# The two V products with the meta keys of an attention unit, side by side on 64 rows each, behind the K products

## The reference

```
s_grid = einsum('bqhd,bkqjhd->bhqkj', q_r, k_r) * scale + bias
s_meta = einsum('bqhd,bmhd->bhqm', q_r, km) * scale + mbias
p = softmax(concatenate([s_meta, s_grid], axis=-1))
out = einsum('bhqm,bmhd->bqhd', p_m, vm) + einsum('bhqkj,bkqjhd->bqhd', p_g, v_r)
# layer: h = rms_norm(x); u, g_pool, q, k, v, g_na = split(h @ w_in)
# y = rms_norm(x + concat([pool(u) * silu(g_pool), out * silu(g_na)]) @ w_out)
```

## Time and profile before

| | us |
|---|---|
| runs of the kernel | 1765.36, 1771.95, 1772.95 (median 1771.95) |
| the profiled execution | 1772.99 |
| its span on the slowest core (core 3) | 1771.5 |
| spans of the other cores | 1756.9 to 1767.5 |
| PE busy in the span | 1697.0 (96%) |
| DVE, ACT busy in the span | 1001.9 (57%), 821.2 (46%) |

### The profile page before, as it was taken

How to read it: one execution, slowest core, us unless ns; L and a number is a source line. 1 busy time by engine, 2 the same in 40 slices (tenths; PEclk the granted TensorE clock), 3 DMA queues, 4 the chain that set the end, 5 groups by cost and what they waited for, 6 DMA issues and landing times.

```text
span 1771.5 us, 39313 instructions; the slowest of 8 cores (1756.9 to 1771.5 us)
## 1 busy us (share of the span) xinstructions
PE 1697.0 (96%) x13906; PEld 875.6 (49%) x13906; DVE 1001.9 (57%) x1907; ACT 821.2 (46%) x1219; POOL 114.7 (6%) x186
## 2 busy tenths in 40 slices
PE   7799999999999999999999889899999999999998
PEld 3344544444455555555555554344444444444443
DVE  3354544442466675666667665456655566556654
ACT  3356666331266765677666662223333233323332
POOL 1011021111100000000000110000000000000000
PEclk9899999999999999999999999899999999999999
DMA  9689778653555566666533448853466336642421
GB/s 249 228 221 291 228 238 240 199 169 137 171 138 156 147 177 177 150 185 180 148 108 107 151 133 235 217 140 102 105 173 173 100 92 154 173 138 98 111 95 60
DMA packets 157446, 287.63 MB, mean 162 GB/s; under 512 B 63235, under 2 KB 85251, under 8 KB 148679
## 3 DMA queue, kind: packets, MB, share of 16 engines
q1 hardware_dynamic: 106103, 157.66, 31.3%
q0 software_dynamic: 34880, 91.46, 18.8%
q10 hardware_dynamic: 16272, 35.99, 6.6%
HBM read 193.33 MB, written 100.90 MB: 166 GB/s over the span
## 4 chain that ended last, share of the span: by engine, by line
PE 79%; DMA 6%; ACT 4%; issue 4%; SPq 3%; DVE 3%; ACTq 0%; DVEq 0%; POOL 0%; POOLq 0%
PE bankpair L427 17%; PE bankpair L403 9%; PE bankpair L612 8%; PE bankpair L889 8%; PE bankpair L580 8%; PE bankpair L376 8%; PE bankpair L908 8%; PE bankpair L1016 4%; PE bankpair L985 4%; ACT sb_PT L991 2%; DMA at_s<-sb_ATT 2%; DMA sb_XSG<-xt 1%; SPq L471 1%; SPq L350 1%; PE bankpair L1004 1%
## 5 line engine op out<-in xcount | busy, mean ns | idle before, releaser
L991 ACT ACTIVATE sb_PT<-bankpair 128x1024 bf16<-128x1024 f32 (+1 forms) x368 | 318.9, 921 | 162.7 <-PE bankpair L985 105.8
L427 PE MATMUL bankpair<-sb_Wo,sb_MIX 128*128 128x512 bf16 x1536 | 333.6, 379 | 0.0
L427 PEld LDWEIGHTS bankpair<-sb_Wo,sb_MIX 128*128 128x128 bf16 x1536 | 150.2, 98 | 181.5 <-issue 0.7
L997 DVE TENSOR_TENSOR sb_PT<-sb_PT,sb_FT 128x1024 bf16<-128x1024 bf16 (+1 forms) x264 | 175.4, 667 | 114.0 <-ACT sb_PT L991 111.5
L908 PE MATMUL bankpair<-sb_Wz,sb_HT 128*128 128x512 bf16 x768 | 201.3, 386 | 3.6 <-ACT sb_PM L934 2.8
L580 PE MATMUL bankpair<-sb_HT,sb_Wk 128*128 128x512 bf16 (+1 forms) x832 | 191.2, 385 | 8.3 <-ACT sb_Wk L215 3.9
L889 PE MATMUL bankpair<-sb_HT,sb_Wq 128*128 128x512 bf16 x768 | 191.8, 380 | 1.9 <-DVE sb_QT L213 1.7
L376 PE MATMUL bankpair<-sb_HT,sb_Wg 128*128 128x512 bf16 x768 | 186.4, 387 | 5.9 <-DVE sb_Y L430 4.7
L612 PE MATMUL bankpair<-sb_Wv,sb_HT 128*128 128x512 bf16 x816 | 184.0, 379 | 0.0
L433 ACT ACTIVATE sb_junk<-sb_Y 128x1024 bf16<-128x1024 f32 x48 | 50.7, 1056 | 273.4 <-DVE sb_Y L430 273.4
L403 PE MATMUL bankpair<-sb_HT,sb_Wg 128*128 128x512 bf16 x768 | 167.7, 379 | 0.0
(11 more groups left out here) (103 smaller groups left out, 1707.2 us busy)
## 6 DMA issues: line engine op xcount, KB each, us to landing
sb_X<-xall SPq DMA_DIRECT2D x51, 512.0 KB, 6.6
sb_XR<-xall SPq DMA_DIRECT2D x48, 512.0 KB, 5.2
y<-sb_O POOLq DMA_DIRECT2D x48, 512.0 KB, 4.9
sb_HT<-hT_s SPq DMA_DIRECT2D x23, 1024.0 KB, 6.7
sb_KR<-kT_s SPq DMA_DIRECT2D x14, 1024.0 KB, 7.7
sb_UW<-u_s SPq DMA_DIRECT2D x54, 256.0 KB, 7.7
kT_s<-sb_KTs POOLq DMA_DIRECT2D x13, 1024.0 KB, 5.0
v_s<-sb_Vs POOLq DMA_DIRECT2D x49, 260.0 KB, 3.6
```

Source lines behind the costliest of these rows:

```text
L427: S.op('tensor', lambda e, po=po, kc=kc, cg=cg, j=j: e.matmul(banks[po][:, :], MIX[:, kc, j * 128:(j + 1) * 128], Wo[kc // 4][:, kc % 4, c ...
L991: S.op('scalar', lambda e: e.activation(out=PT[ps][0:nk, bi, :, 0:n].rearrange('p (a b) q -> p a b q', a=2), in_=bank2[sp][0:nk, :].rearra ...
L997: S.op('vector', lambda e: e.tensor_tensor(out=PT[ps][0:nk, bi, :, 0:n], in0=PT[ps][0:nk, bi, :, 0:n], in1=bl['E'](hs), op=ALU.mult), read ...
```

## The change

The heads are split over the banks in another way: bank 4 holds the first half of the unit's eight heads (jj 0 and 1, both parities), bank 5 the second half. The 16 meta keys of each head stand on 16 rows of PM and VMb, in such an order that half 0 needs the rows 0 to 63 and half 1 the rows 64 to 127. So the meta product of a half contracts over 64 rows only; both are issued one after the other, directly behind the K products of a pair, at one point per unit that `pv_plan` chooses: in the third step's pair where the unit during which they run has 3 or 4 blocks and is even, in the second step's pair for 3 blocks and odd, in the first for 2 blocks. A meta product no longer opens bank 4 in the first two cases; the first grid product does.

The portions of V products move too. For an even unit of 3 or 4 blocks, half 0 runs in the steps 0 and 1 and all of half 1 in step 2, behind the norm of half 0. Before, the first two blocks of the second bank ran in step 1. For units of 2 blocks the portions stay, without the meta products in between. The V products with the combined block VC now always contract over 128 rows; where only 64 carry data, a memset on DVE (four in all) clears the other rows of VC.

```diff
-                def p2_pvmeta(ui, par):
+                def p2_pvmeta(ui, opens, ends=False):
...
+                    for half in range(2):
+                        rows = slice(64 * half, 64 * half + 64)
+                        S.op('tensor', lambda e, half=half, rows=rows: e.matmul(
+                            banks[4 + half][:, 0:260], PM[t % 2][rows, G, s, :], VMb[rows, G, 0:260],
+                            start=(opens or half == 1), stop=(ends and half == 0)), reads=[('PM', t % 2, G)] + VMR, writes=[PS(4 + half)])
...
-                def pv_steps(ui):
-                    nb = len(unit_blocks(units[ui]))
-                    steps = [[], [], []]
-                    steps[0].append(lambda: p2_pvmeta(ui, 0))
-                    for bi in range(nb - 1):
-                        steps[0].append(lambda bi=bi: p2_pv(ui, 0, bi, False))
-                    steps[1].append(lambda: p2_pv(ui, 0, nb - 1, True))
-                    steps[1].append(lambda: p2_norm(ui, 0))
-                    steps[1].append(lambda: p2_pvmeta(ui, 1))
-                    for bi in range(nb):
-                        steps[1 if bi < 2 else 2].append(lambda bi=bi: p2_pv(ui, 1, bi, bi == nb - 1))
-                    steps[2].append(lambda: p2_norm(ui, 1))
-                    return steps
+                def pv_plan(ui):
...
+                    even = ui + 1 == len(units) or first_step[ui + 1] % 2 == 0
+                    opens = even and nn == 2
+                    lead = [lambda bi=bi: p2_pv(ui, 0, bi, bi == 0 and not opens, False) for bi in range(nb - 1)]
+                    tail = lambda last: [lambda: p2_pv(ui, 0, nb - 1, False, last)]
+                    half1 = [lambda bi=bi: p2_pv(ui, 1, bi, False, bi == nb - 1) for bi in range(nb)]
+                    n0, n1 = [lambda: p2_norm(ui, 0)], [lambda: p2_norm(ui, 1)]
+                    if nn == 2:
+                        return 0 if even else 1, opens, {0: lead, 1: tail(True) + n0 + half1 + n1}
+                    if even:
+                        return 2, False, {0: lead, 1: tail(False), 2: n0 + half1 + n1}
+                    return 1, False, {0: lead, 1: tail(True) + n0 + half1[:2], 2: half1[2:] + n1}
...
                         p2_qk(ui, b)
                     for ui, b in steps[k:k + 2]:
+                        if ui > 0 and pv_plan(ui - 1)[0] == b:
+                            p2_pvmeta(ui - 1, pv_plan(ui - 1)[1], b == 2)
+                    for ui, b in steps[k:k + 2]:
                         unit_step(ui, b)
```

More of the change, by code:

```diff
@@ L857, in build_program @@
                         S.op('sync', lambda e, jj=jj, par=par, p0=p0: e.dma_start(
[L858 removed]
+                            out=VMb[p0:p0 + 16, :, (2 * (jj % 2) + par) * 65:(2 * (jj % 2) + par) * 65 + 65],
                             in_=v_d[VM + 16:VM + 32, :].rearrange('m (g q f) -> m g q f', g=2, q=8)[:, :, 2 * jj + par, :]),
@@ L962, in unit_blocks @@
                         b = dict(nk=nk, parts=[(i, 7 * w, 1, 64 * k) for k, i in enumerate(tl['ch'])], V=VC[w],
-                                 vres=[('VC', w, k) for k in range(len(tl['ch']))])
+                                 vres=[('VC', w, k) for k in range(2)])
                         if tl['xs'] is None:
@@ L1086, in unit_step @@
                             late.pop(0)()
-                    for f in pv_steps(ui - 1)[b] if ui > 0 and b < 3 else []:
+                    for f in pv_plan(ui - 1)[2].get(b, []) if ui > 0 else []:
                         f()
-                    if nb == 2 and b == 1 and ui > 0:
-                        for f in pv_steps(ui - 1)[2]:
-                            f()
                     if b == nb - 1:
```

46 lines of the change are left out of this document (24 added, 22 removed).

## The result

| | before | after |
|---|---|---|
| time, median, us | 1769.25 | 1821.59 |
| ratio to before, 95% interval | | 1.0285 (1.0251 to 1.0320) |
| the profiled execution, its span, us | 1772.99, 1771.5 | 1822.29, 1820.6 (core 1) |
| phase 2, slowest core (median of the 8 cores), us | 610.1 (608) | 660.6 (657) |
| phases 1 and 3, slowest core, us | 456.3, 696.3 | 456.5, 694.7 |

The prediction was 1826, with a range of 1798 to 1852. The kernel is 2.9% slower and its median is 4.4 us under the forecast. Most of that is the base: the forecast adds 53 us to the profiled execution of 1772.99, and the ratio says that 50 us were added to a median of 1769.25.

A forecast was written before the change was run, and what follows sets the result against it. PE was taken to bound phase 2, busy 578.75 of 610.5 us. Sum: 1772.99 - 10.6 - 1.1 - 7 + 43 + 19 + 10 = 1826 us, range 1798 to 1852.

The forecast's parts named there:

- The 24 waits of half 1: In the A2-B0 pairs, half 1's first V product waits for DVE's multiplication of B0: 43 us lost.
- The 14 waits of tiles 0 and 4: Meta products opening both banks behind the K products wait for both norms of the unit before: 19 us lost.
- The pair and the changes of rows: Meta products side by side gain 10.6 us; fewer 128-to-64-row changes at V products with VC gain 1.1 us.
- The old waits: Existing 11.4 us of waits at meta products partly vanish behind the K products: 7 us gained.
- The clock: In phase 2, new long waits lower PE's granted clock about ten times, 1.0 us each: 10 us lost.
- the third rival: Clock falls after each long wait, 34 us in place of 10: 1850 us, chance 0.10.
- the first: Rival: V products of half 1 start without new waits and only the gain remains: 1754 us, chance 0.04.
- The second: Rival: A's first V products wait only for the bank, 1.1 us 24 times, 26 in place of 43: 1804, chance 0.10.
- The fourth: Rival: the meta products don't run side by side, no gain of 10.6: 1837 us, chance 0.05.
- the sign of an error: Wrong if L1019 doesn't wait for L1000, its waits name L1035 (the bank), or phase 2 isn't what changes.

The follow-up runs named there:

- experiment 1: Changed kernel, but unit B at s = 0 of two-chunk tiles writes its blocks to PT slots 3, 0, 1, not 0, 1, 2: 1813.46 us, ratio 1.0239.
- experiment 3: Changed kernel, but in two-block units (tiles 0 and 4) step 1's V products and norms stand ahead of its filling: 1809.24 us, ratio 1.0211.
- experiment 7: Changed kernel, but in two-block units (tiles 0 and 4) the meta pair stands behind the first filling, not the K products: ratio 1.0230.
- experiment 8: As experiment 6, but two-block units defer the meta pair to the next pair's K products, closing both banks, norms ahead of that pair's multiplications: ratio 1.0017.
- experiment 9: As experiment 8, but half 0's norm is issued ahead of the multiplications in even units of 4 blocks too: ratio 0.9995.
- experiment 5: Changed kernel, but in 24 units half 1's first two blocks run in step 1, before B0 is written; the meta pair closes both banks: 1812.92 us.
- experiment 10: As experiment 9, but both meta products of a pair use rows 0 to 63: ratio 1.0045.
- experiment 2: Changed kernel, but even 3-block units have V products in earlier places and the meta pair opens both banks behind their first pair's K products: 1824.51 us.
- experiment 6: As experiment 5, but in those 24 pairs half 0's norm is issued on DVE ahead of the multiplications of A2 and B0: 1791.51 us, ratio 1.0108.

## Why the prediction was right

Point by point, phase 2 of the slowest core, 610.1 to 660.6:

- **The 24 waits of half 1** were put at 43 us and measured 39.3; shown as a wait for the slot by experiment 1. (That the list's entry is 42.9 is chance: the 24 have 35.4 us of it, since the list leaves out the modelled end of the product before, and the 13 others 7.5.) The single ones: 1.80 with four products of filling (1.9 predicted), 1.58 with five (1.67), 2.0 in tile 3, 1.8 and 2.5 in tile 12. The sign and nearly the whole of the size rest on this term.
- **The 14 waits of tiles 0 and 4** were put at 19 and measured 18.5; experiments 3, 7 and 8 take most or all of them away and gain 10 to 16 us.
- **The pair and the changes of rows** were put at -11.7. The undisturbed distances sum to 493.5 before and 487.1 after, so -6.4. The products run side by side even better than taken (4 ns apart, 0.112 us for the pair with the change behind it taken out, 0.125 taken), but a change was not seen: behind the 20 pairs of 64*64 K products the pair starts 148 ns after the last of them, and behind 64*128 ones 52 ns. In the rows above: 830.36 to 830.94 and another 0.21 to the filling, where before the filling itself came 0.58 after the K products. That the pair "adds no such change" was wrong for these, about 3 us in all with the narrow tiles. The rest is in the V products, a term that the prediction put at nothing ("cost the same there and here"). The mean distance from one V product to the next, distances over 45 ns left out, went from 30.9 to 32.1 ns on each of the eight cores, and is 32.0 to 32.2 in every experiment: about 3 us over 2626 such distances. Which part of the new order of heads makes them dearer is not shown.
- **The old waits** were put at -7. Outside the 38 new waits, V and meta products lose 13.5 us (51.4 - 39.3 + 19.9 - 18.5) against 16.9 before: -3.4. They did not vanish with the meta products' old places; as the prediction said of part of them they passed to the first grid products. In the list these are the other 13 of the 37 waits of L1019, 0.2 to 1.4 us each, 11 of them in tiles 12 and 13; each product starts 0.15 us after a norm's multiplication (L1035) has ended.
- **The clock** was put at +10, ten more stretches at the lower level. The stretches of phase 2 at a granted clock of 0.50, counted whole, have 27.3 us against 17.1: 10.2 us more, of which at most half is lost, 5 us. Seven stretches stand against five. Most waits of 1.6 to 1.8 us left the clock at 1.00, and some stretches at 0.50 follow waits of K products for ACT. So the third rival (1850) is out and the term was at least twice too large.

The sum by the measured terms is -6.4 - 3.4 + 39.3 + 18.5 + 5 = 53 against 50.5. Without the clock it is 48.0, which leaves 2.5 us for the clock and for everything else. The mechanism, the sign and the largest terms were right; that the total of +53 came so close was luck, since the smaller terms were off in both directions: the gain 5.3 too large, the old waits 3.6, the new ones 4.2 too large and the clock 5.

Of the rivals, the first (a gain alone) asks that the waits be gone: experiments 8 and 9 come nearest to that kernel and are level with the kernel before, not 18.7 us faster; but V and meta products still wait 27.3 us in experiment 9 against 16.9 before, so the rival's condition is not met in full. The second was shown by experiment 5 to be the next wait in line. The fourth is out by experiment 10. Of what I named as the sign of an error, the list of waits does name a norm (L1033) and not L1000 for the 24 waits. The timeline and experiment 1 show that it is the name and not the cause that is off.

The Trainium skill, TensorEngine Tiling, section Theoretical Speedup, gives up to 2x for a small dimension of at most 64; here two 260-column products on 64 rows each cost 0.11 us together, where one on 128 rows cost 0.11. The Trainium skill, TensorEngine Tiling, section Key Properties, says that changing the tiling mode drains the engine, without limiting this to the number of rows; the 96 ns between 64*64 and 64*128 agree with that.

Where the pair's remaining gain goes in experiment 9 can be read from its trace. PE has 8 us less to do there (485.5 against 493.5), but on the slowest core V and meta products wait 10.4 us more than before (27.3 against 16.9); the difference of the two is the 2.4 us by which its phase 2 is longer. In the median of the eight cores these waits are 23.4 against 15.6 us, so they take 7.8 of the 8 us there too. The commonest is the second meta product behind the norm that frees bank 5, 0.49 us each time. That phase 2 is still 5 us shorter in the median of the cores is made up elsewhere and stays open; the time differs by less than can be measured.

## What to carry to other kernels

When work moves behind a producer of the next item that writes the same buffer, it reads the new item's values, and a wait for that producer which was not in the order before is the sign of it: look at the order first. The wait is not free either, even if the engine is the bound: compare the time at which the queue gets there with the end of that write, and look at what the next instruction in line waits for too, since taking one wait away only uncovers it (experiments 1 and 5). Two products side by side need both of their destination banks at once; in this kernel it was cheaper to let them close banks that were already open than to open them (experiments 5 and 8 against 2). And put the instruction that frees a bank ahead of longer work on its engine: experiment 6 moved one norm ahead of two multiplications and gained 19 us over experiment 5.

## What the runs showed of the hardware that was not expected

- Two products of 260 columns on the two halves of the rows start 3 to 4 ns apart; on the same half 111 ns, the cost of a full 128-row product.
- A change between two tilings with 64 rows (64 and 128 columns of the array) costs 96 ns (148 against 52 from the last K product to the pair), about as much as one between 64 and 128 rows (125 from a V product to a K product, 29 to 33 from one V product to the next).
- A V product that waited for DVE starts 0.145 to 0.15 us after the end of the DVE instruction, in all traces read.
- V products of the same size came at other distances when the heads were taken in another order: 30.9 ns before, 32.1 after, on all eight cores. The cause is open.
- Most waits of 1.4 to 2.5 us between dense stretches did not lower the granted clock. Of the 21 of this length at half 1, two were followed by a stretch at 0.50, which began 0.1 and 1.4 us after the product had started (at 1044.25 and 1078.38, in tile 12). The stretch that begins 0.8 us before the end of the wait at 833.83 has 1.00; the one at 822.38, behind waits of K products for ACT, has 0.50 (columns as in the earlier trace rows):

```profile
822.38:825.79 3.41, 3.41 (x29) 1.73 (x26) 3.19 (x8) 1.56 (x2) 0.00 (x0) 0.50 0.45 161
...
833.00:836.41 3.41, 2.58 (x52) 1.93 (x53) 2.56 (x7) 1.34 (x3) 0.00 (x0) 1.00 0.49 142
1044.25:1047.66 3.41, 3.41 (x41) 2.22 (x40) 0.96 (x3) 1.22 (x2) 0.88 (x1) 0.50 0.97 293
1078.38:1081.79 3.41, 3.41 (x56) 1.97 (x50) 1.75 (x5) 3.40 (x7) 0.90 (x2) 0.50 0.62 148
```
